# Feed-forward inner rows computed transposed in a two-layer hybrid decoder trunk, fp32 from high and low parts

## The reference, cut to what matters

```python
x = x + 0.5 * swiglu(rmsnorm(x, ffn1_norm), w_gate, w_up, w_down)   # inner width 2816
h = rmsnorm(x, mix_norm)
proj = h @ w_in                       # q, k, v of three mixers, three gate groups
ya, yb, yc = attn_a @ w_a, attn_b @ w_b, attn_c @ w_c    # 256, 256, 512 inner rows
x = x + (sig(g_a)*ya + sig(g_b)*yb + sig(g_c)*yc) @ w_out
x = x + 0.5 * swiglu(rmsnorm(x, ffn2_norm), ...)
# swiglu(x) = (silu(x @ w_gate) * (x @ w_up)) @ w_down
```

## Time and profile before

| | |
|---|---|
| median of 3 runs | 1172.64 us (1172.56 to 1172.72) |
| profiled execution | 1172.3 us, its span 1170.5 us |
| PE matmul / weight load busy | 1156.0 us (99%) / 950.7 us (81%) |
| DVE / ACT / POOL busy | 688.5 us (59%) / 607.1 us (52%) / 81.8 us (7%) |
| weight splits on DVE, L1053 | 388 of 1230 ns |
| DMA | 206.99 MB, 177 GB/s in the mean |
| instruction fetches, queue q8 | 29 packets, 0.48 MB |

### The profile page before, as it was taken

One profiled execution on the slowest core, in us unless ns is written; L12 is line 12 of the kernel. 1 busy time (PEld: TensorE's weight loads), 2 busy tenths in 40 slices (PEclk: granted clock), 3 DMA queues, 4 the chain that ended last, 5 costly groups with the idle time before them and its releaser, 6 DMA issues.

```text
span 1170.5 us, 15735 instructions
## 1 busy us (share of the span) xinstructions
PE 1156.0 (99%) x5459; PEld 950.7 (81%) x5459; DVE 688.5 (59%) x944; ACT 607.1 (52%) x920; POOL 81.8 (7%) x89
## 2 busy tenths in 40 slices
PE   8999999999999999999999999999999999999998
PEld 6888887888887888888788888878878878888886
DVE  5554555878656665544565554467786476554553
ACT  6544444656773554444454444456577735444441
POOL 3100000210101000000040000002110010000000
PEclk9999999999999999999999999999999999999999
DMA  9955553544535565556566555626454436656510
GB/s 306 312 175 194 192 189 122 180 145 148 175 145 180 180 216 182 182 177 212 179 156 216 181 181 183 208 87 203 144 176 149 178 112 205 224 180 213 181 72 36
DMA packets 138339, 206.99 MB, mean 177 GB/s; under 512 B 6818, under 2 KB 99028, under 8 KB 138292
## 3 DMA queue, kind: packets, MB, share of 16 engines
q1 hardware_dynamic: 137444, 205.55, 52.8%
q0 software_dynamic: 752, 0.79, 0.8%
q10 hardware_dynamic: 96, 0.02, 0.0%
HBM read 205.29 MB, written 1.05 MB: 176 GB/s over the span
## 4 chain that ended last, share of the span: by engine, by line
PE 96%; DVE 2%; ACT 1%; issue 1%; ACTq 0%; DVEq 0%; POOLq 0%; POOL 0%
PE bank L486 30%; PE bank L490 30%; PE bank L489 30%; PE bank L550 2%; PE bank L500 1%; PE bank L666 1%; PE bank L636 1%; PE bank L652 1%; PE bank L651 1%; PE bank L680 0%; PE bank L681 0%; PE bank L682 0%; DVE work L1296 0%; PE bank L557 0%; DVE probs L1219 0%
## 5 line engine op out<-in xcount | busy, mean ns | idle before, releaser
L1053 DVE TENSOR_TENSOR w_low<-raw,w_high 128x1024 fp32r<-128x1024 f32 x388 | 466.8, 1230 | 228.9 <-ACT w_high L810 228.2
L810 ACT ACTIVATE w_high<-raw 128x1024 fp32r<-128x1024 f32 x388 | 402.1, 1057 | 242.7 <-PE bank L490 132.4
L486 PE MATMUL bank<-w_high,xT_high 128*128 128x512 f32 (+1 forms) x1152 | 456.1, 396 | 1.3 <-DVE xT_low L1071 0.6
L490 PE MATMUL bank<-w_low,xT_high 128*128 128x512 f32 (+1 forms) x1152 | 446.5, 388 | 0.0
L489 PE MATMUL bank<-w_high,xT_low 128*128 128x512 f32 (+1 forms) x1152 | 445.3, 387 | 0.0
L486 PEld LDWEIGHTS bank<-w_high,xT_high 128*128 128x128 f32 x1152 | 216.5, 188 | 48.6 <-issue 7.2
L490 PEld LDWEIGHTS bank<-w_low,xT_high 128*128 128x128 f32 x1152 | 216.3, 188 | 45.4
L489 PEld LDWEIGHTS bank<-w_high,xT_low 128*128 128x128 f32 x1152 | 216.8, 188 | 40.8
L486 PE MATMUL bank<-w_high,hT_high 128*128 128x512 f32 x352 | 137.6, 391 | 3.2 <-DVE hT_low L1102 3.2
L490 PE MATMUL bank<-w_low,hT_high 128*128 128x512 f32 x352 | 137.0, 389 | 0.0
L489 PE MATMUL bank<-w_high,hT_low 128*128 128x512 f32 x352 | 137.0, 389 | 0.0
(11 more groups left out here) (120 smaller groups left out, 688.3 us busy)
## 6 DMA issues: line engine op xcount, KB each, us to landing
raw<-in_w_in SPq DMA_DIRECT2D x92, 512.0 KB, 4.5
raw<-in_ffn_w_down SPq DMA_DIRECT2D x88, 512.0 KB, 4.0
raw<-in_ffn_w_gate SPq DMA_DIRECT2D x87, 512.0 KB, 4.0
raw<-in_ffn_w_up SPq DMA_DIRECT2D x87, 512.0 KB, 5.0
raw<-in_w_out SPq DMA_DIRECT2D x16, 512.0 KB, 4.1
raw<-in_w_branch_c SPq DMA_DIRECT2D x8, 512.0 KB, 3.7
raw<-in_w_branch_a SPq DMA_DIRECT2D x4, 512.0 KB, 3.7
raw<-in_w_branch_b SPq DMA_DIRECT2D x4, 512.0 KB, 3.7
```

The source lines that it names most:

```text
L486: first = nc.tensor.matmul(out, left_high, w_high[:, slot, cols], start=start, stop=False)
L490: return nc.tensor.matmul(out, left_high, w_low[:, slot, cols], start=False, stop=stop)
L810: act.activation(w_high[:, slot], raw[:, in_slot, (p % 2) * 1024:(p % 2) * 1024 + 1024], ACT.Copy).then_inc(sem["high_ready"], 1)
L1053: dve.tensor_tensor(w_low[:, slot], raw[:, FILL_SLOT[p // 2], (p % 2) * 1024:(p % 2) * 1024 + 1024], w_high[:, slot].bitcast(F32), ALU.sub ...
```

## The change: what it does

- Gate and up are computed transposed: 128 columns of a weight block are stationary, and the turned x moves. High and low x lie side by side in one tile `xT`, so one pass with the high weights takes 512 columns (high x into columns 0 to 255 of a bank, low x into 256 to 511), and one with the low weights takes 256 columns of high x. A chunk uses banks 0 to 3, one for each 128 inner rows (gate, gate, up, up); every chunk uses the same four.
- ACT copies each bank's second half to SBUF (`copy_rest`), DVE adds it to the first (`scale_gate`, `multiply_hidden`), multiplies the gate by a row of norm factors, ACT takes silu, DVE multiplies by up and 0.5. No turn follows; `hidden_high` and `hidden_low` work from SBUF into `oT_high`, `oT_low`. Up isn't scaled by the norm factor: `residual` multiplies by it instead of 0.5.
- Once per feed-forward PE turns `norm_scale` into a row (`turn_row`, two transposes ahead of the fourth pair) and ACT copies it (`copy_row`).
- In a feed-forward's first pair the passes that need only high x come first (12 of 256 columns, then 4 of 256 and 4 of 512), with the wait for the low part between them. Its two groups of turned x use banks 4, 5 and 6, 7 instead of 2, 3.
- Next chunk's PE waits for `gate_summed` and `up_summed` before it writes the banks again.
- Branches run in the order B, A, C; C is done quarter by quarter over its four steps (`last_pairs(..., count=4)`). POOL's addition becomes DVE's.
- The chunk loops of PE, ACT and DVE are written out; SP's stays a loop.

```diff
@@ gate_up_pair (PE)
+                def full(k, n):
+                    return nc.tensor.matmul(bank[n][:, :], w_high[:, slot, column(k, n)], xT[:, k], start=k == 0, stop=False)
+                def high_part(k, n, weights=w_low, start=False):
+                    return nc.tensor.matmul(bank[n][:, 0:S], weights[:, slot, column(k, n)], xT_high[:, k], start=start, stop=k == KB - 1)
...
+                if low_wait:
+                    for n in range(4):
+                        one = high_part(0, n, w_high, True)
+                        if n == 0 and release:
+                            one.then_inc(sem["pair_used"], release)
+                    for k in pair:
+                        for n in range(4):
+                            high_part(k, n)
+                    low_wait()
+                    for n in range(4):
+                        low_part(0, n)
+                    for n in range(4):
+                        last = full(1, n)
+                else:
+                    for n in range(4):
+                        if j == 0 and n == 0:
+                            pe.wait_ge(sem["gate_summed"], value("gate_summed", layer, chunk - 1))
+                        if j == 0 and n == 2:
+                            pe.wait_ge(sem["up_summed"], value("up_summed", layer, chunk - 1))
+                        for k in pair:
+                            one = full(k, n)
+                            if n == 0 and k == pair[0] and release:
+                                one.then_inc(sem["pair_used"], release)
+                            last = high_part(k, n)
+                        if j == 3 and n == 1:
+                            last.then_inc(sem["gate_done"], 1)
@@ chunk (PE)
-                        if n == HIDDEN_TURN:
-                            turn_hidden(layer, done, (2 * j, 2 * j))
@@ branches (PE)
-                for k in range(2):
-                    wide_pair(layer, p + k, oT_high, oT_low, 4 + k, k == 0, release=1 - k)
-                last_pairs(layer, p + 2, oT_high, oT_low, 6, False)
+                last_pairs(layer, p, oT_high, oT_low, 2, True, release=1)
...
-                last_pairs(layer, p + 6, oT_high, oT_low, 2, True, turn_merged, quarter_free, release=2)
+                last_pairs(layer, p + 4, oT_high, oT_low, 4, True, turn_merged, quarter_free, release=2, count=4)
@@ copy_rest, silu_gate, hidden_high (ACT)
+                act.wait_ge(sem["gate_done"], value("gate_done", layer, chunk))
+                act.activation(gate_scaled[:, :, :], banks[:, 0:2, S:2 * S], ACT.Copy).then_inc(sem["rest_copied"], 1)
                 act.wait_ge(sem["gate_up_done"], value("gate_up_done", layer, chunk))
+                act.activation(up_sum[:, :, :], banks[:, 2:4, S:2 * S], ACT.Copy).then_inc(sem["rest_copied"], 1)
+                act.wait_ge(sem["gate_scaled"], value("gate_scaled", layer, chunk))
+                act.activation(silu[:, :, :], gate_scaled[:, :, :], ACT.Silu).then_inc(sem["silu_ready"], 1)
@@ ffn_chunks (ACT), DVE alike with row_ready, scale_gate, multiply_hidden
-                            if n == SILU_AT:
-                                silu_gate(layer, i * 2 + (before + 1 + j), j, 3 if before else 1)
+                            if n == (ROW_AT if i == 0 and j == 0 else SILU_AT):
+                                if i == 0 and j == 0:
+                                    copy_row(layer, 2 if before else 1)
+                                copy_rest(layer, i * 2 + (before + 1 + j))
+                                silu_gate(layer, i * 2 + (before + 1 + j))
@@ scale_gate, multiply_hidden (DVE)
+                dve.tensor_tensor(gate_scaled[:, :, :], banks[:, 0:2, 0:S], gate_scaled[:, :, :], ALU.add).then_inc(sem["gate_summed"], 1)
+                dve.drain()
+                dve.tensor_tensor(gate_scaled[:, :, :], gate_scaled[:, :, :], norm_row[:, :].unsqueeze(1).to_broadcast([P, 2, S]), ALU.mult
+                                  ).then_inc(sem["gate_scaled"], 1)
...
+                dve.tensor_tensor(up_sum[:, :, :], banks[:, 2:4, 0:S], up_sum[:, :, :], ALU.add).then_inc(sem["up_summed"], 1)
+                dve.drain()
+                dve.wait_ge(sem["silu_ready"], value("silu_ready", layer, chunk))
+                dve.scalar_tensor_tensor(hidden[:, :, :], up_sum[:, :, :], 0.5, silu[:, :, :], ALU.mult, ALU.mult
+                                         ).then_inc(sem["hidden_ready"], 1)
@@ merge_a (DVE); merge_c is the same with gate(2, n), merge_b one multiplication
+                dve.wait_ge(sem["product_done"], value("product_done", layer, 8 + n + 1))
+                dve.tensor_tensor(scratch[:, n % 2], a_quarter(*QUARTERS[n])[:, :], gate(0, n), ALU.mult)
+                dve.drain()
+                dve.tensor_tensor(merged_quarter(n), merged_quarter(n), scratch[:, n % 2], ALU.add)
```

More of the change, by code:

```diff
@@ L163, in build @@
         work = sb("work", [P, 2048])
[L164 to L167, removed]
+        silu, hidden, gate_scaled, up_sum = (work[:, 512 * n:512 * n + 512].rearrange("p (f s) -> p f s", f=2) for n in range(4))
+        norm_row = sb("norm_row", [P, S])
         qk_raw = [work[:, 1024 * b:1024 * b + 1024].rearrange("p (t c) -> p t c", t=HALVES) for b in range(2)]
@@ L194, in build @@
             [stats[:, i, n] for n in range(2)] for i in range(6))
-        bank = [ctx.enter_context(nc.psum_tensor(f"bank{b}", [P, 512], F32)) for b in range(8)]
+        banks = ctx.enter_context(nc.psum_tensor("bank", [P, 8, 512], F32))
+        bank = [banks[:, b] for b in range(8)]
         sem = {name: ctx.enter_context(nc.semaphore(name)) for name in PER_LAYER}
@@ L472, in _ @@
                 scale_context(layer)
[L474 to L477, removed]
                 norm(layer, 3)
@@ L525, in wide_pair, with last_pairs @@
                 last.then_inc(sem["pair_used"], 1)
-            def last_pairs(layer, p, high, low, kb, start, before_last=None, before=None, block=None, release=0, banks=quarter):
-                pe.wait_ge(sem["low_ready"], value("low_ready", layer, p + 2))
+            def last_pairs(layer, p, high, low, kb, start, before_last=None, before=None, release=0, banks=quarter, count=2):
+                pe.wait_ge(sem["low_ready"], value("low_ready", layer, p + count))
                 for n, (half, cols) in enumerate(QUARTERS):
@@ L543, in last_pairs, with turn_row @@
                     last.then_inc(sem["product_done"], 1)
[L545 to L552, removed]
+            def turn_row(layer, n):
+                pe.wait_ge(sem["norm_ready"], value("norm_ready", layer, n))
+                for half in range(HALVES):
+                    last = nc.tensor.transpose(bank[4][:, half * P:half * P + P], norm_scale[:, half:half + 1].to_broadcast([P, P]),
+                                               ident[:, :])
+                last.then_inc(sem["row_turned"], 1)
             def warm(count):
@@ L601, in ffn @@
                 done = chunks_before + CHUNKS
[L602 to L608, removed]
+                pe.wait_ge(sem["hidden_low"], value("hidden_low", layer, done))
+                last_pairs(layer, first + FFN_PAIRS - 2, oT_high, oT_low, 0, False, after)
             def proj_pair(layer, chunk, j, release):
@@ L881, in ffn_chunks @@
                 act.drain()
-                with act.Fori(0, (CHUNKS - 1) // 2) as i:
+                for i in range((CHUNKS - 1) // 2):
                     for j in range(2):
@@ L1074, in blocks_low, with residual @@
                     last.then_inc(sem["blocks_low"], 1)
-            def residual(layer, n, product, factor):
+            def residual(layer, n, product, normed):
                 half, cols = QUARTERS[n]
@@ L1080, in residual @@
                 v = x[:, half, 512 * cols:512 * cols + 512]
-                dve.scalar_tensor_tensor(v, quarter(half, cols)[:, :], factor, v, ALU.mult, ALU.add
+                dve.scalar_tensor_tensor(v, quarter(half, cols)[:, :], norm_scale[:, half:half + 1] if normed else 1.0, v, ALU.mult, ALU.add
                                          ).then_inc(sem["residual_done"], 1)
-            def multiply_hidden(layer, chunk, odd):
-                for half in range(HALVES):
-                    dve.wait_ge(sem["silu_ready"], value("silu_ready", layer, 2 * chunk + (half - 1)))
-                    last = dve.scalar_tensor_tensor(hidden[:, half], bank[2 * odd + half][:, FC:2 * FC], norm_scale[:, half:half + 1],
-                                                    silu[:, half], ALU.mult, ALU.mult)
-                last.then_inc(sem["hidden_ready"], 1)
@@ L1105, in ffn_chunks, with hidden_low @@
+            def hidden_low(layer, chunk, buf):
+                dve.wait_ge(sem["hidden_high"], value("hidden_high", layer, chunk))
+                dve.tensor_tensor(hT(oT_low, buf), hidden[:, :, :], hT(oT_high, buf).bitcast(F32), ALU.subtract
+                                  ).then_inc(sem["hidden_low"], 1)
             def ffn_chunks(layer, first, before):
```

(2 more changed lines are left out.)

187 lines of the change are left out of this document (90 added, 97 removed).

## The result

The changed kernel takes 1165.48 us (median of 4 runs, 1165.22 to 1165.71) against 1172.62 before: ratio 0.9940, 95% interval 0.9926 to 0.9953. It is faster, by 7.1 us. Forecast were 14.1. The profiled execution took 1165.29 us.

A forecast was written before the change was run, and what follows sets the result against it. PE, busy 99% of the span at full clock, was taken to bound the kernel through the pitch of its matmul starts. Terms summed to -14.15 us: 1172.3 to 1158.15, with 0.34 added 1158.5 us; 8-in-10 range 1150 to 1169.

The forecast's parts named there:

- step 1: Gate/up: 48 matmuls of 512 become 32 of 512 and 32 of 256, at 227 and 120 ns; +9.2 and +0.2 us.
- Step 2: Turns between chunks, four transposes on PE: 0.446 us each, forty of the 44 go; -17.8 us.
- Step 3: A feed-forward's last chunk: 1.49 us between two down steps goes, four times, without a new wait; -5.9 us.
- Step 4: Row of norm factors: two transposes on PE, 0.23 us, four times, source ready before; +0.9 us.
- Step 5: A feed-forward's edges: first pair no longer waits for low x, -0.95 us; transposes at the end, -0.4 us.
- Step 6: PE's waits for gate and up sums: none in ordinary chunks, +0.5 at three second chunks, +1.9 at the first; +3.4 us.
- Step 7: Branches: PE's waits for B's addition and a late weight split go, +0.2 at C's last quarter; -2.8 us over two layers.
- Step 8: Residual's factor, straight code for the loops, POOL's additions gone, weight transfers: claimed to change nothing.
- A: Half passes in gate/up are dear, the next full pass's load lacking cover; gain gone at 10 ns each, up to 1254; chance 0.07.
- B: One set of banks: PE loses 0.3 us twice in 40 chunks waiting for ACT and DVE; +24.8, 1183 us; chance 0.06.
- C: Longer chains at feed-forward edges: late hidden low and first sums, +1 us four times each; 1166.5 us; chance 0.15.
- D: Half passes in gate/up run at 109 ns like the transposes; 15.5 us less, 1143 us; chance 0.07.

The follow-up runs named there:

- 384 columns: The changed kernel with each half pass taking 384 columns of x instead of 256, same order; 1236.7 us (one run).

## Why the prediction was right and wrong

The direction was right and the time lies in the range, but the gain was half of the forecast. The failed step is 1, its last sentence: "I take 120, from the row with the same width, the same kind of data and a load each time." That row is of 256-column passes among themselves. In the ordinary chunk's mixture a full pass doesn't keep its 227 ns: it takes 236 on average, and the half pass 117, where step 1 had 347 for both and 353.3 were measured. Here is the loss by order in ordinary chunks, for two full and two half passes (693.3 ns nominal: 2 x 226.7 + 2 x 120), from the starts inside gate and up; a whole chunk is 16.535 nominal, and the down steps after the last half pass start late too:

| order | ns over nominal | chunk, us | time, us |
|---|---|---|---|
| full, half, full, half | 13.3 | 16.793 | 1165.5 |
| two and two | 3 | 16.586 | 1157.5 |
| full, half, half, full | 3 | 16.586 | 1157.7 |
| four and four | 8.4 | 16.686 | 1162.0 |
| eight and eight | 4.9 | 16.613 | 1163.8 (edges late) |
| one width (all 512, all 256) | 0 | 19.95, 16.98 | 1299.0, 1174.0 |

What is shown: in ordinary chunks the time depends on the order of widths, and not on the bank, the operand that moves or the room to hide a load. But a change of width has no price of its own: S falls too, since 31 couples at 25.79 and again at 599.93 ran at the nominal 347 ns in the slowest order of all. Which of the two patterns a stretch had could be seen from its third couple on, and it stayed to the end of the stretch. After half passes the first five full passes start 7, 8, 2, 5 and 4 ns late (eights: 234, 235, 229, 232, 231, then 227), and the first half pass after a full one comes 7 ns early. What stays open is why runs of two are the cheapest, and what picks the pattern: the second chunks of all four feed-forwards start after a wait for the same sum, and two pay while two don't. Nothing in the trace shows the unit that this comes from.

The size: 0.22 us a chunk over the forecast's 16.57, in the 36 ordinary chunks, is 7.9. The two second chunks that pay add 0.4; the other two and the first chunks add next to nothing. That is 8.3 of a miss of 7.1 (1165.29 against 1158.15). The rest went the other way by 1.2: 0.4 at the branches' last quarter, where no wait came; 0.4 at the sums (1.67 + 3 x 0.43 = 3.0 for 3.4); 0.2 in the kernel's first chunk, where steps 1 and 4 put 0.4 ahead of the fourth pair, which waits for its weights anyway and starts at 20.92 for 20.71 before. The last 0.2 I can't assign.

Point by point. Step 2: the turns and their 0.45 us are gone. Step 3: right, no wait, by its rows. Step 4: right, the two transposes and the slower start after them cost 0.22 in the later three feed-forwards, where 0.23 was forecast; in the first they lie in the wait for weights. Step 5: right, 0.95 forecast and 1.1 measured by itself. Step 6: right, 25.35 forecast and 25.36 seen at the first edge, though it cost 1.67 and not 1.9, as the pair before it ended later than forecast; ordinary chunks don't wait for the sums. Step 7: 2.8 forecast, 3.1 measured by itself. Step 8: nothing seen.

Of the rivals, A was the right place with the wrong mechanism: its break-even was 10 ns a half pass, 6.7 were paid in ordinary chunks, and not for the load, as 384 columns and the chunks without loss showed. The rule of the Trainium skill's section Part 3 in "TensorE: Matmul & The Clock Gate", that loads overlap only matmuls of another row group, is not borne out: by it a load would come on top of a 256-column pass's 107 ns of columns, and with 96 of them in a chunk, each with a load, a pass with its load took 120 ns in all. B fell: no ordinary chunk has idle time ended by L1114. C and D weren't needed; the smaller gain came from the pitch and not from the edges.

The version with pairs of passes beats both: 1157.5 us, 8.0 less than the changed kernel and 15 less than before, by one added line of code.

## What to carry to other kernels

A pitch read from a stretch of equal matmuls holds for equal matmuls. Where a change mixes widths, bound the mixture by a few ns a pass and multiply by the count: 7 ns a couple took half the gain here. Try the order of the passes first; of the four run lengths tried, two of each width was best. And work out the edges from the queues' order, since they were right to some 0.2 us a place where every duration had a row.

## What the runs showed of the hardware

- A full pass of 512 columns in a row of its like starts 226.7 ns after the one before, one of 256 columns 120 ns, whichever operand moves: 13.3 ns over the columns at the full clock, in both. In alternation 1224 couples cost 353.3 ns each, 6.7 more than the two alone, and 152, nearly all of the first chunks and of two second chunks, 347, no more than the two alone.
- In ordinary chunks the loss depends on the order: 13.3, 3, 8.4 and 4.9 ns for four passes in runs of one, two, four and eight.
- After eight half passes five full ones start late, some 27 ns in all. After the alternation of an ordinary chunk the down steps start late for longer: in the changed kernel the ten starts from 103.68 on took 2.33 us instead of 2.27. Narrower matmuls do the same: in the kernel before, the nine starts of 512 columns from 29.73 on, after a turn, took 2.09 us instead of 2.04.
